# A one-core kernel of a whole forward pass: the first part of sparse attention is reordered, constant products are put before some waits of TensorE, and the decay products get full rows

## The reference, cut to what matters

```python
# first block
h = rms_norm(x);  u = h @ w_in
y_a = short_conv_mixer(u)          # gates times a causal convolution
y_g = gated_deltanet_mixer(u)      # chunks of 64 tokens, a triangular solve, states
y_n = nsa_mixer(u)                 # sparse attention: compressed, selected and window keys
x += sum(sigmoid(h @ w_gate + b_gate) * branches(y_a, y_n, y_g)) @ w_out
x += hier_moe(rms_norm(x))         # 32 experts of width 512, two per token
# second block: shift, scale and gate from mod = silu(c) @ ada_w[i] + ada_b[i]
x += g1 * mla_mixer(h)             # latent attention, 16 heads
x += g2 * swiglu(h)                # feed-forward, width 2816
x += g1 * mamba2_mixer(h)          # state space, 32 heads, 4 groups
x += g2 * moe_swiglu(h)            # 8 experts of width 2816, two per token
return rmsnorm(x)
```

## Time and profile before

| what | value |
|---|---|
| median of 3 runs | 2529.43 us (2526.84 to 2530.20) |
| the profiled execution: its time | 2528.53 us |
| its span | 2526.7 us |
| its mean granted clock of TensorE | 0.924 |
| TensorE busy | 2146.5 us (85%) |
| TensorE loading weights | 1622.4 us (64%) |
| VectorE busy | 1424.3 us (56%) |
| ScalarE busy | 1157.9 us (46%) |
| GpSimd busy | 40.9 us (2%) |
| moved from and to memory | 656.69 MB, mean 260 GB/s |

### The profile page before, as it was taken

The page is one execution under the profiler, slowest core; times in us unless marked ns, Lnnn a source line. Parts: engine busy times, 40 slices in busy tenths (PEclk is TensorE's granted clock), DMA queues, the critical chain, the costliest instruction groups (busy, mean ns, idle before and its releaser), DMA issues.

```text
span 2526.7 us, 29676 instructions
## 1 busy us (share of the span) xinstructions
PE 2146.5 (85%) x12223; PEld 1622.4 (64%) x12223; DVE 1424.3 (56%) x1976; ACT 1157.9 (46%) x1520; POOL 40.9 (2%) x107
## 2 busy tenths in 40 slices
PE   6889788876656656887999988879999999999997
PEld 6867566652111111566997867668787787887875
DVE  3844435421111101434455666658889888888997
ACT  4432244310000000443443556538777787777775
POOL 0000100000000000000000000000000000000000
PEclk9989898879888888997999888889999999999999
DMA  8451651469999999476445322238989989989994
GB/s 265 167 182 69 234 199 56 178 253 408 409 409 409 409 409 402 165 267 234 151 183 183 112 90 99 84 125 293 362 323 329 373 324 359 339 314 371 332 335 189
DMA packets 267692, 656.69 MB, mean 260 GB/s; under 512 B 13456, under 2 KB 38548, under 8 KB 267546
## 3 DMA queue, kind: packets, MB, share of 16 engines
q1 hardware_dynamic: 266592, 652.90, 69.6%
q10 hardware_dynamic: 952, 1.77, 0.2%
HBM read 653.60 MB, written 1.05 MB: 259 GB/s over the span
## 4 chain that ended last, share of the span: by engine, by line
PE 68%; DMA 16%; DVE 9%; ACT 4%; issue 2%; POOL 0%; ACTq 0%; DVEq 0%; POOLq 0%; SPq 0%
PE psum L257 17%; PE psum L258 17%; PE psum L259 16%; PE psum L252 9%; DMA ring<-in_w_expert_up 5%; DMA ring<-in_w_expert_down 5%; DMA ring<-in_w_expert_gate 5%; PE psum L2344 2%; DVE w_lo L202 2%; PE psum L1086 1%; ACT w_hi L192 1%; PE psum L879 1%; PE psum L2366 1%; DMA ring<-in_ada_w 1%; DVE xbc L885 1%
## 5 line engine op out<-in xcount | busy, mean ns | idle before, releaser
L202 DVE TENSOR_TENSOR w_lo<-ring,w_hi 128x1024 fp32r<-128x1024 f32 (+1 forms) x778 | 905.0, 1178 | 399.7 <-ACT w_hi L192 384.6
L192 ACT CAST w_hi<-ring 128x1024 fp32r<-128x1024 f32 (+1 forms) x778 | 785.2, 1015 | 442.9 <-PE psum L259 438.6
L257 PE MATMUL psum<-w_hi,xg_hi 128*128 128x512 f32 (+1 forms) x768 | 294.7, 384 | 1.3 <-ACT xg_lo L2027 1.3
L259 PE MATMUL psum<-w_lo,xg_hi 128*128 128x512 f32 (+1 forms) x768 | 289.5, 377 | 0.0
L258 PE MATMUL psum<-w_hi,xg_lo 128*128 128x512 f32 (+1 forms) x768 | 289.5, 377 | 0.0
L2344 PE MATMUL psum<-ring,hT 128*32 128x512 f32 x960 | 149.7, 756 | 114.6 <-DMA ring<-in_w_expert_gate 64.8
L2344 PEld LDWEIGHTS psum<-ring,hT 128*32 128x32 f32 x960 | 29.8, 126 | 229.4 <-issue 79.0
L257 PEld LDWEIGHTS psum<-w_hi,xg_hi 128*128 128x128 f32 x768 | 144.8, 189 | 31.1 <-issue 1.7
L258 PEld LDWEIGHTS psum<-w_hi,xg_lo 128*128 128x128 f32 x768 | 144.9, 189 | 29.4 <-issue 1.7
L259 PEld LDWEIGHTS psum<-w_lo,xg_hi 128*128 128x128 f32 x768 | 144.7, 188 | 29.2
L257 PE MATMUL psum<-w_hi,midT_hi 128*128 128x512 f32 x352 | 140.8, 400 | 3.9 <-DVE w_lo L202 3.9
(11 more groups left out here) (662 smaller groups left out, 3722.7 us busy)
## 6 DMA issues: line engine op xcount, KB each, us to landing
ring<-in_moe_w_gate SPq DMA_DIRECT2D x40, 2048.0 KB, 9.3
ring<-in_moe_w_up SPq DMA_DIRECT2D x40, 2048.0 KB, 10.0
ring<-in_moe_w_down SPq DMA_DIRECT2D x40, 2048.0 KB, 9.2
ring<-in_w_expert_gate SPq DMA_DIRECT2D x30, 2048.0 KB, 17.5
ring<-in_w_expert_up SPq DMA_DIRECT2D x30, 2048.0 KB, 17.6
ring<-in_w_expert_down SPq DMA_DIRECT2D x30, 2048.0 KB, 17.8
ring<-in_ada_w SPq DMA_DIRECT2D x24, 2048.0 KB, 8.9
ring<-in_ssm_w_in SPq DMA_DIRECT2D x10, 2048.0 KB, 8.0
```

Source lines behind the costliest of these rows:

```text
L192: a.copy(self.buffers(n, src.shape)[0], src).then_inc(*self.hi_made.up())
L202: v.tensor_tensor(lo, src, hi.bitcast(F32), SUB).then_inc(*self.lo_made.up())
L257: p.matmul(o, l[0], r[0], start=start, stop=False)
L259: return p.matmul(o, l[0], r[1], start=False, stop=stop)
```

## The change

1. **Constant products.** A new function writes products of the identity with itself into the first 128 columns of a PSUM pair. They are put before some 20 waits of TensorE, in the numbers of the table. The bank is taken before the wait instead of after it where both stood together.
2. **Sparse attention's first part.** Ada pair 3 moves into the gated-delta stage, before "oT"; pair 4 goes behind projection 0, pair 5 behind merge step (2, 3), and its turn behind attention. VectorE makes `dup` as soon as projection 1 is there, and its transposes "kcT" come directly behind the projections; merge steps (2, 0) and (2, 1) move ahead of the waits for `fl` and `h1`; the transposes of queries and keys move behind "h1T". The ring's order, ScalarE and VectorE follow: the norm is cut into squares and multiplications, and the additions for `fl` come before the keys' norms.
3. **Decays.** `csT` has 128 rows, 96 of them zero, and the product goes over all 128.

| before which wait | products |
|---|---|
| norm of mix, moe1, mla, ffn, ssm, moe2 | 9, 18, 11, 24, 24, 22 |
| first convolution unit | 18 |
| "thin"; behind "rows"; "LT"; "oT" (gated delta) | 15; 12; 16; 10 |
| steps `len(jobs)` and the next of each attention | 5 each |
| "ynT" (end of sparse attention) | 4 |
| turned and first unit of the output projection | 13, 6 |
| places of the first experts | 20 |
| turned and first unit after latent attention | 4, 6 |
| "dt"; first "xs" | 7; 20 |
| "ysum" of groups 0 to 3 | 0, 10, 13, 4 |
| first pair step of the second experts | 6 |

```diff
+def constant_products(p, o, constant, n):
+
+    for _ in range(n):
+        p.matmul(o[:, 0:P], constant[:, :], constant[:, :], start=True, stop=True)
...
+    ada_units(0, 3, 4)
     columns_unit(("nsa", 0), w_in, O_Q, 512, row_parts(512))
     columns_unit(("nsa", 1), w_in, O_KV, 512, row_parts(512))
+    ada_units(0, 4, 5)
     columns_unit(("nsa", 2), w_in, O_KV + 512, 256, row_parts(256))
     gate_unit(2, 0)
-    ada_units(0, 3, ADA_PAIRS)
     for j in range(2):
         columns_unit(("cmp", j), A["cmp_w1"][0][j], 0, 256)
     branch_unit(2, 0)
     gate_unit(2, 1)
+    ada_units(0, 5, ADA_PAIRS)
     branch_unit(2, 1)
...
         ada_pe(p, 0, 2)
+        ps = banks.take(p, "LT")
+        constant_products(p, ps, ident, 16)
         p.wait_ge(*st.dve.of("L"))
-        ps = banks.take(p, "LT")
...
+        ada_pe(p, 0, 3)
+        ps = banks.take(p, "oT")
+        constant_products(p, ps, ident, 10)
         p.wait_ge(*st.dve.of("o"))
-        ps = banks.take(p, "oT")
...
                 ins.then_inc(*st.pe.up("out", m))
+                if len(jobs) <= n < len(jobs) + AHEAD:
+                    constant_products(p, ps[:, 512:1024], ident, 5)
...
             by_token_pe(p, u, h_mix, [[ps[:, t * 512:t * 512 + w] for t in range(NT)]])
-        ada_pe(p, 0, 3)
-        ada_pe(p, 0, 4)
-        ada_turn_pe(p, 0, 3)
-        ada_pe(p, 0, 5)
-        ada_turn_pe(p, 0, 4)
-        p.wait_ge(*st.dve.of("normed"))
...
+            if n == 0:
+                ada_turn_pe(p, 0, 3)
+                ada_pe(p, 0, 4)
         p.wait_ge(*st.dve.of("dup"))
         ps = banks.take(p, "kcT")
...
+        ada_turn_pe(p, 0, 4)
+        merge_step_pe(p, 2, 0)
         p.wait_ge(*st.dve.of("fl"))
...
-        ada_turn_pe(p, 0, 5)
-        merge_step_pe(p, 2, 0)
+        merge_step_pe(p, 2, 1)
         p.wait_ge(*st.dve.of("h1"))
         ps = banks.take(p, "h1T")
         transposes(p, ps, [h1]).then_inc(*e.up("h1T"))
-        merge_step_pe(p, 2, 1)
+        p.wait_ge(*st.dve.of("normed"))
...
         merge_step_pe(p, 2, 3)
+        ada_pe(p, 0, 5)
         p.wait_ge(*st.act.of("vc"))
         attention_pe(p, st, nsa_s, nsa_pT, nsa_jobs, beside=merge_beside_pe)
+        ada_turn_pe(p, 0, 5)
...
     def decays_pe(p, h):
         ps = banks.take(p, "decay", h)
-        product(p, ps[:, 0:T], [(ident[0:32, h:h + 1].to_broadcast([32, P]), csT[:, :])]).then_inc(*S["ssm"].pe.up("decay", h))
+        product(p, ps[:, 0:T], [(ident[:, h:h + 1].to_broadcast([P, P]), csT[:, :])]).then_inc(*S["ssm"].pe.up("decay", h))
```

VectorE's part of the new order in `nsa_dve`:

```diff
-        for n in range(3):
-            split.make_lo(v, min(split.end(unit["nsa", n]) + PARTS, cap))
-        v.wait_ge(*st.act.of("proj", 2))
-        nsa_norm_dve(v, q, 0, 8, gains[:, 0, :], 64.0 ** -0.5, 0)
-        nsa_norm_dve(v, kv, 256, 2, gains[:, 2, :], 1.0, 8)
-        nsa_norm_dve(v, kv, 512, 2, gains[:, 3, :], 1.0, 10)
+        split.make_lo(v, min(split.end(unit["nsa", 1]) + 1, cap))
+        v.wait_ge(*st.act.of("proj", 0))
+        ada_turn_dve(v, 0, 3)
+        nsa_squares_dve(v, q, 0, 8, 0)
+        split.make_lo(v, min(split.end(unit["nsa", 1]) + PARTS, cap))
+        v.wait_ge(*st.act.of("proj", 1))
         for jg in range(4):
             for c in range(2):
                 v.tensor_copy(dup[:, jg, :, 64 * c:64 * c + 64], kv[:, :, 64 * jg:64 * jg + 64]).then_inc(*d.up("dup"))
-        ada_turn_dve(v, 0, 3)
-        ada_turn_dve(v, 0, 4)
+        nsa_squares_dve(v, kv, 256, 2, 8)
+        split.make_lo(v, min(split.end(unit["nsa", 2]) + PARTS, cap))
+        nsa_norm_dve(v, q, 0, 8, gains[:, 0, :], 64.0 ** -0.5, 0)
         v.memset(fl[:, :, :, 30:32], 0.0).then_inc(*d.up("fl"))
         v.wait_ge(*st.act.of("kcT"))
...
-        ada_turn_dve(v, 0, 5)
+        v.wait_ge(*st.act.of("proj", 2))
+        nsa_squares_dve(v, kv, 512, 2, 10)
+        merge_step_dve(v, 2, 0)
+        ada_turn_dve(v, 0, 4)
+        nsa_norm_dve(v, kv, 256, 2, gains[:, 2, :], 1.0, 8)
+        nsa_norm_dve(v, kv, 512, 2, gains[:, 3, :], 1.0, 10)
         v.wait_ge(*st.act.of("h1"))
```

More of the change, by code:

```diff
@@ L319, in __init__ @@
         self.n_k = F // P
+        self.idle = 20 if name == "1" else 0
 class Run:
@@ L590, in block @@
     daT = sb("daT", [32, T], where=sm)
-    csT = sb("csT", [32, T], where=sm)
+    csT = sb("csT", [P, T], where=sm)
     cs = sb("cs", [P, NT, 32], where=sm)
@@ L993, in mix_pe @@
         st = S["mix"]
-        norm_pe(p, st, xn_mix)
-        p.wait_ge(*st.dve.of("h", 0))
+        norm_pe(p, st, xn_mix, 9)
         for n in range(3):
-            by_feature_pe(p, unit["conv", n], h_mix, ready=None if n else st.dve.of("h", 4))
+            by_feature_pe(p, unit["conv", n], h_mix, ready=None if n else st.dve.of("h", 4), begin=None if n else st.dve.of("h", 0), idle=0 if n else 18)
         for n in range(4):
@@ L1266, in gdn_pe @@
         e = st.pe
+        ps = banks.take(p, "thin")
+        constant_products(p, ps, ident, 15)
         finished(p, S["mix"])
         p.wait_ge(*small.end())
-        ps = banks.take(p, "thin")
         for t in range(NT):
@@ L1701, in nsa_act @@
             banks.empty(e, "unit", u)
-        for n in range(3, ADA_PAIRS):
-            ada_act(a, 0, n)
+            if n == 0:
+                ada_act(a, 0, 4)
+        a.wait_ge(*st.pe.of("kcT"))
+        a.copy(kcT[:, :, :].rearrange("p h t -> p (h t)"), banks.of("kcT")).then_inc(*e.up("kcT"))
+        banks.empty(e, "kcT")
+        merge_step_act(a, 2, 0)
+        a.wait_ge(*st.pe.of("cmp"))
+        a.copy(h1, banks.of("cmp")[:, 0:P]).then_inc(*e.up("h1"))
+        banks.empty(e, "cmp")
+        a.wait_ge(*st.dve.of("h2"))
+        a.activation(h2, h2, ACT.Sigmoid, scale=2.0 * math.sqrt(2.0 / math.pi)).then_inc(*e.up("h2"))
+        a.wait_ge(*st.pe.of("h1T"))
+        a.copy(h1T[:, :, :].rearrange("p n c -> p (n c)"), banks.of("h1T")[:, 0:P]).then_inc(*e.up("h1T"))
+        banks.empty(e, "h1T")
         for h0 in (0, 4):
@@ L1750, in nsa_norm_dve @@
                    d, "squares", k0)
+    def nsa_norm_dve(v, buf, c0, n, gain, scale, k0):
+        st = S["nsa"]
+        d = st.dve
+        heads = buf[:, :, c0:c0 + 64 * n]
         v.wait_ge(*st.pool.of("rn", k0))
@@ L1941, in places_pe @@
         n = M.n_exp
+        ps = banks.take(p, st.name, "places")
+        constant_products(p, ps, ident, M.idle)
         p.wait_ge(*st.dve.of("some"))
-        ps = banks.take(p, st.name, "places")
         product(p, ps[:, 0:n], [(upper[:, :], M.some[:, 0, :])])
@@ L2011, in pair_step_pe @@
         h, k0 = h_rows[step // 2], 4 * (step % 2)
+        ps = banks.take(p, "pair", j, step)
+        if j == 0 and step == 0:
+            constant_products(p, ps, ident, 6)
         p.wait_ge(*st.dve.of("rows"))
         p.wait_ge(*st.dve.of("sel_pair", j))
-        ps = banks.take(p, "pair", j, step)
         for k in range(4):
@@ L3048, in ssm_pe @@
         for t in range(NT):
[L3049 removed]
+            ins = p.transpose(ps[:, t * 32:t * 32 + 32], csT[0:32, t * P:(t + 1) * P], ident[0:32, 0:32])
         ins.then_inc(*e.up("cs"))
@@ L3327, in ssm_dve @@
         v.memset(on32[:, :], 1.0).then_inc(*d.up())
+        v.memset(csT[:, :], 0.0).then_inc(*d.up())
         v.memset(upad2[:, :, :, 0:3], 0.0).then_inc(*d.up("pad"))
```

88 lines of the change are left out of this document (46 added, 42 removed).

## The result

The kernel after takes 2492.61 us (median of 4 runs, 2489.03 to 2494.04) against 2529.81 us for the kernel before (median of 4): the ratio is 0.9852, with a 95% interval of 0.9835 to 0.9869. That is 37 us less, where 58 were forecast; it lies inside the range of 2450 to 2508. The profiled execution took 2489.03 us (span 2487.2), 39.5 us less than that of before; it is the fastest of the four.

The account below looks back on a forecast made before the run. TensorE's chain and its half clock bound the kernel. Clock and decays less costs, 46.5 us, less 4.5 and 5, leave 37; with 21 for the reordering, 58 off 2529 gives 2471 us, range 2450 to 2508 (forecast's own 2455 to 2485).

Parts of the forecast that it names:

- rival (b): The products don't hold the clock up; reordering without its clock part and the decays stay: 2511 us, chance 0.11.
- The reordering: Sparse attention's first part: first scores at 329.4 instead of 350.9 us, a gain of 21 us, bounds 10 to 25.
- Rival (a): The reordering gives a third, as fl or the ada loads wait elsewhere: 2485 us, chance 0.10.
- The clock sites: Places where TensorE's chain runs at half clock: time there less time at full clock, summing to 46.5 us.
- Latent attention: norm 0.5: Clock site at latent attention's norm: a gain of 0.5 us from running at the full clock.
- the two next groups 4.0, the last group's ... 5.0 of 7.5: Clock sites in the state-space groups: gains of 4.0 us and, in the 20.5 us stretch, 5.0 of 7.5 us.
- LT: minus 1.6: Cost at "LT": 16 products stand before a TensorE wait of only 0.37 us: minus 1.6 us, 6.5 at half clock.
- The attention tails' 2.2: Cost of five products in two late steps of each attention: minus 2.2 us in the sparse one, 0 in latent.
- The decays: Decays over 128 instead of 32 rows have records below 400 ns: gain 3.8 us, bounds 0 to 6.6.
- Rival (c): Half of the clock gain is off the path: 2490 us, chance 0.12.
- Rival (e): Transposes don't hold the clock, so the norms fall back by 8 us: 2479 us, chance 0.02.
- (d): Slower: the products run at half clock and outlast their waits, 38 us against 25 gained: 2542 us, chance 0.04.

Follow-up runs that it names:

- norms_full: start_plus3 with 8 more products before each of four norms (first experts, feed-forward, state space, second experts): 2488.02 us, ratio 0.9826.
- ysum_ahead: The kernel after with the 10, 13 and 4 state-space group products put ahead of the bank's wait: 2488.74 us, ratio 0.9833.
- joined: The kernel after with start_plus3, mla_norm_none, ysum_ahead and lt_moved together: 2475.89 us, ratio 0.9783.
- mla_norm_none: The kernel after without the 11 products before latent attention's norm: 2488.55 us, ratio 0.9833.
- start_plus3: The kernel after with 12 instead of 9 products before the first norm: 2485.25 us, ratio 0.9822.
- lt_moved: The kernel after with the 16 products of "LT" moved behind the transposes of L, k and v, into the wait for XT: 2488.93 us, ratio 0.9833.
- thin_products: The kernel after with every constant product over 32 rows of the identity instead of 128: 2523.0 us, ratio 0.9973 to the kernel before.
- reorder_only: The kernel after with no constant products and the decays back at 32 rows: 2509.66 us, ratio 0.9919 to the kernel before.
- no_products: The kernel after with no constant products, decays kept at 128 rows: 2504.11 us, ratio 0.9895 to the kernel before.
- ysum_none: The kernel after without the 10, 13 and 4 products at the starts of state-space groups 1 to 3: 2493.89 us, ratio 0.9846.

## Why the prediction was right, and where it was not

The forecast was 21 us too low. The range holds the time because it reached up to near rival (b); the mechanisms are right, two sites and the decays are not.

**What bounds the kernel** was right: TensorE's chain and its clock. Busy TensorE time grew and the total fell.

**The reordering** was right in size and mechanism: 20 us alone, against 21. The two DMA waits are gone, the one new wait is for `fl` (7.1 us against 8), and from oT's transposes to the first scores it takes 73.4 us (257.34 to 330.72), 71.3 by the prediction's sum and 92.8 before. Rival (a) falls.

**The clock sites** were right in kind: 98 of 245 us of half clock are gone, the experts' loop passed the lead on unchanged (28.1 us before it, 28.4 behind), and rival (b) falls. Their sum was too high: TensorE's work at half clock fell from 188.7 to 126.0 us, which by the prediction's own halving is worth 31 us, not 46.5. The prediction took each stretch to the full clock and took off 4.5 us for waits that stay idle in part. `norms_full` shows that the clock falls again at the next gap, so one place's gain can be the next place's loss; `ysum_ahead` and `joined` show it again at the second experts. At the first experts 4.7 of 8.5 us came: the logits are at the full clock (3.77 us), the transposes (3.59) and most of the gather (5.47) are not.

**Two steps failed outright.** "Latent attention: norm 0.5": it lost 8.5 us. About 4 of them are the eleven products, which run after x is ready (`mla_norm_none`); the rest is the end of the code block that the longer code moved to this place (`start_plus3`). And for the groups "the two next groups 4.0, the last group's ... 5.0 of 7.5": the prediction read the wait for `xs` and didn't ask what stands ahead of the products in the changed order. `banks.take` does, with its own wait for z, nearly as long. Placed ahead of it, they bring 6.5 us (`ysum_ahead`), of 11.2 that are missing in that row of the table. The rest isn't assigned; and as 13 of the 20 decays that gain by full rows lie in this row and 7 in the one above it, the clock's part fell short by more than the table shows. These two places are 20 of the 28 us between the sum before discounts and the result.

**The costs.** "LT: minus 1.6" was right (`lt_moved`). The other half of the 3.2 us lost there is a step that was missing: the lead of the start sites, 3.6 us, is TensorE's alone, and L is made by VectorE. The attention tails' 2.2 was right to a tenth (2.25 us).

**The decays** were near in number (3.8 us, and 5.5 came) by luck: the step was wrong. "The 32-row form takes 486 ns, the 96-row form 383": over 128 rows the record still takes 476 ns. At the full clock alone the 32-row records of the kernel before average 425 ns, so 61 of the 103 ns were the clock of their stretches, which the 96-row form never met. What full rows save is the 0.32 us before the next product, at the 20 decays shown above. It isn't in the prediction at all.

**The rivals.** Rival (c) names nearly the time that came (2490), but not its reason: it had half of the clock's gain off the path. In the table the lead of each site is still there at the end, and what is missing sits at the two places above. Rival (e) falls too: in `joined` the clock is at half from 979.4 to 986.2 us, TensorE runs nothing but the norm's 16 transposes in that time, and behind them the clock is full. (d) has the mechanism that `thin_products` shows; in the kernel after it happened at single places only (20 records of products in 4.6 us at latent attention's norm and at group 1).

## What to carry to other kernels

Work that is only there to hold the clock has to stand ahead of every wait of its gap, the accumulator's own included, and it has to use full rows: with 32 rows it cost 19 us instead of giving 12. Where the gap lies behind a branch, the engine may be waiting for its code; filler there was pure cost, and a change in the length of code far ahead moved 5 us there. A product over 32 rows among products over 128 delays its neighbour, though its own record is no longer; fill its rows with zeros. Judge such sites one at a time by the distance between two fixed instructions, since the clock's falls move from gap to gap and single totals hide what one site does; then look at the next gaps too.

## What the runs showed of the hardware that was not expected

- Constant products over 32 instead of 128 rows take nearly as long (5.74 against 5.52 us for 48 records) but hold TensorE's clock worse: 228.7 against 147.1 us at 1.2 GHz.
- A 32-row product between products over 128 rows delays the next one: it starts 0.62 us behind a 32-row decay and 0.30 us behind a 128-row one, at the full clock, though the records take 479 and 476 ns (`reorder_only`, `no_products`).
- Behind a taken branch TensorE stood for 3.5 us (kernel after) and 5.1 us (`start_plus3`) until code arrived, and in the kernel after for 5.2 us more at the end of that block, 4 instructions on. It went on 1.3 to 1.4 us behind the landing of an instruction packet (kernel after, `mla_norm_none`).
- Identical code differed by up to 4 us at the first scores (330.72, 334.56 and 334.83 us in the kernel after, `ysum_ahead` and `ysum_none`), because one ada pair ran at 3.66 or at 6.5 us, by where the clock's fall met it.
